# Latent rows of batch 0 between the norm turns of both batches, latent turns under rows, first gate under the rope

## The reference, cut to what matters

```python
h = rms_norm(x, norm_g[1])
proj = h @ w_in                                   # 1024 -> 384 + 256 + 32 + 1024
c_q, c_kv, k_rope, gate = jnp.split(proj, [384, 640, 672], axis=-1)
q  = rms_norm(c_q, q_norm_g) @ w_q_up             # later stage
kv = rms_norm(c_kv, kv_norm_g) @ w_kv_up          # later stage
k_rope = apply_rope(k_rope, cos, sin)
y = o * jax.nn.silu(gate)                         # later stage
```

## Time and profile before

| | us |
|---|---|
| median of 3 runs (1814.23 to 1816.08) | 1815.68 |
| the profiled execution's own time | 1816.16 |
| its span, first to last instruction | 1814.4 |
| `stage_b_in` in it: DVE's first instruction to its last | 1175.65 to 1369.76 |
| PE's first transpose to its last matmul there | 1177.38 to 1364.56 |
| span of PE busy, whole kernel | 1729.9 (95%) |

### The profile page before, as it was taken

How to read it: one execution, slowest core, us unless ns; L and a number is a source line. 1 busy time by engine, 2 the same in 40 slices (tenths; PEclk the granted TensorE clock), 3 DMA queues, 4 the chain that set the end, 5 groups by cost and what they waited for, 6 DMA issues and landing times. The chain is left out here.

```text
span 1814.4 us, 24638 instructions
## 1 busy us (share of the span) xinstructions
PE 1729.9 (95%) x8720; PEld 1462.7 (81%) x8720; DVE 1107.5 (61%) x1974; ACT 726.2 (40%) x1465; POOL 400.8 (22%) x320
## 2 busy tenths in 40 slices
PE   6999999999999999999999999698997999999995
PEld 5888888888888888888888887588786788888883
DVE  5354365456455455455455445544797888888986
ACT  5223223313312322312322322333215877777774
POOL 1001001001001001001000100211004877777774
PEclk9999999999999999999999999898899999999997
DMA  4112112111111112011111110020100000000002
GB/s 162 47 35 70 35 35 70 36 35 58 35 46 58 35 35 68 24 46 58 35 35 70 35 47 1 7 94 1 47 23 27 27 27 26 26 26 26 6 7 110
DMA packets 23241, 76.75 MB, mean 42 GB/s; under 512 B 3088, under 2 KB 3216, under 8 KB 22928
## 3 DMA queue, kind: packets, MB, share of 16 engines
q1 hardware_dynamic: 23184, 75.98, 12.3%
HBM read 71.77 MB, written 4.19 MB: 42 GB/s over the span
## 5 line engine op out<-in xcount | busy, mean ns | idle before, releaser
L754 PE MATMUL bankA<-hTh,wh 128*128 128x512 f32 x1280 | 504.9, 394 | 0.4 <-DVE hTl L504 0.4
L754 PE MATMUL bankA<-hTh,wl 128*128 128x512 f32 x1280 | 498.8, 390 | 0.0
L754 PE MATMUL bankA<-hTl,wh 128*128 128x512 f32 x1280 | 498.8, 390 | 0.0
L754 PEld LDWEIGHTS bankA<-hTh,wl 128*128 128x128 f32 x1280 | 240.4, 188 | 50.9
L754 PEld LDWEIGHTS bankA<-hTh,wh 128*128 128x128 f32 x1280 | 240.7, 188 | 48.3 <-issue 1.1
L754 PEld LDWEIGHTS bankA<-hTl,wh 128*128 128x128 f32 x1280 | 240.8, 188 | 47.0
L304 POOL TENSOR_TENSOR prob<-prob,wt_blk 128x1024 f32<-128x1024 f32 x16 | 32.3, 2022 | 1054.9 <-DVE wt_blk L643 1054.9
L554 DVE TENSOR_TENSOR qk<-bankA,qk 128x512 fp32r<-128x512 f32 x96 | 66.4, 692 | 287.1 <-ACT qk L370 286.9
L370 ACT ACTIVATE qk<-bankA 128x512 fp32r<-128x512 f32 x96 | 57.2, 596 | 366.8 <-PE bankA L754 366.8
L530 DVE TENSOR_TENSOR wl<-raw,wh 128x1024 fp32r<-128x1024 f32 x78 | 103.1, 1321 | 14.5 <-ACT wh L340 12.9
L1475 POOL TENSOR_TENSOR probb<-probb,inv 128x512 f32<-128x512 f32 x96 | 100.0, 1042 | 43.6 <-DVE inv L1666 37.7
(11 more groups left out here) (206 smaller groups left out, 3471.3 us busy)
## 6 DMA issues: line engine op xcount, KB each, us to landing
raw<-a_w_in SPq DMA_DIRECT2D x80, 512.0 KB, 3.3
bias<-alibi SPq DMA_DIRECT2D x8, 512.0 KB, 3.3
raw_out<-a_w_out SPq DMA_DIRECT2D x8, 512.0 KB, 4.1
graw<-b_w_gate SPq DMA_DIRECT2D x8, 512.0 KB, 4.2
raw_o<-b_w_out SPq DMA_DIRECT2D x16, 256.0 KB, 2.6
raw_q<-b_w_q SPq DMA_DIRECT2D x8, 384.0 KB, 3.9
X<-x_prompt SPq DMA_DIRECT2D x4, 512.0 KB, 5.4
X<-x_sample SPq DMA_DIRECT2D x4, 512.0 KB, 8.7
```

Of the source, the lines that this page charges most:

```text
L754: ins = pe.matmul(proj_ps[b][:, :], w[a][:, slot, k * P:(k + 1) * P], hT[c][:, k, b * S:(b + 1) * S], start=(i == 0), stop=(i == last))
```

## The change

PE's new order: norm turns of batch 0; query-latent rows 0 and 1; norm turns 0 to 3 of batch 1; row 2; norm turns 4 to 7 of batch 1; rows 3 to 7; the three query-latent turns of batch 0; all eight key-value rows; gate 0 (of the new order, with both halves); the other seven latent turns; the two rope turns; gates 1 to 7. ACT and DVE follow that order, with one thing to note: what is done with the two halves of gate 0 (exponential, reciprocal, product) stands on both behind the seven other latent turns and the rope's copies. On DVE the rope itself stands ahead of those seven turns.

- The low part of the query-latent weights moves from DVE to POOL, and ACT's split of them from the norm turns of batch 1 to those of batch 0. DVE's first scaling of batch 1 moves from between the norm turns of batch 0 to behind them.
- A row of batch 0 or 1 waits for the norm turns one k at a time (`turn_taken`), not for all eight.
- The weights of the query latent are issued first by SP, the four small tables behind them. The two slots of `graw` go: gate weights are loaded into the part of `gateT` that the gate's own result will take, so the gates run in the order `GATES`, as those parts come free. The first gate's split weights get room of their own behind the key-value weights.

The core of the diff:

```diff
+GATES = (3, 4, 5, 6, 0, 1, 2, 7)
...
-        w = [sb(f"wb{s}", [P, KT * CQ], F32R) for s in "hl"]
+        w = [sb(f"wb{s}", [P, KT * (CKV + B_ROPE) + KT * P], F32R) for s in "hl"]
...
-        latent = scratch[:, 0:NT * CQ].rearrange("p (i c) -> p i c", i=NT)
+        early = sb("early", [P, QT * CQ])
...
-        graw = sb("graw", [P, 2, KT * P])
...
+        gate_at = (KT * widths[1], 0)
...
         @block.sync
         def _(sp):
+            sp.dma_start(raw[:, :], io["b_w_cq"]).then_inc(raw_loaded, 16)
             for dst, name in ((g_col, "g1"), (gq_col, "gq"), (gkv_col, "gkv")):
                 sp.dma_start(dst[:, :], io[name]).then_inc(small_loaded, 16)
             sp.dma_start(rope_tab[:].rearrange("p a j c -> p (a j c)"), io["rope_tok"]).then_inc(small_loaded, 16)
-            sp.dma_start(raw[:, :], io["b_w_cq"]).then_inc(raw_loaded, 16)
-            for n in range(2):
-                sp.dma_start(graw[:, n, :], io["b_w_gate"][n]).then_inc(graw_loaded[n], 16)
...
             sp.wait_ge(w_split, KT)
             sp.dma_start(raw[:, 0:KT * widths[1]], io["b_w_ckv"]).then_inc(raw_loaded, 16)
+            sp.wait_ge(turned, NORM_TURNS)
+            load_gate(3)
...
+            sp.wait_ge(w_split, 2 * KT)
+            load_gate(4)
+            load_gate(5)
+            sp.wait_ge(rope_done, NB)
+            load_gate(6)
+            sp.wait_ge(turned, TR)
+            for n in range(3):
+                load_gate(n)
+            sp.wait_ge(turned, TR + NB)
+            load_gate(7)
...
         @block.gpsimd
...
             pool.memset(key_rope, 0.0).then_inc(zeroed, 1)
+            pool.wait_ge(zeroed, 1)
+            for k in range(KT):
+                cols = slice(k * CQ, (k + 1) * CQ)
+                pool.wait_ge(w_hi, k + 1)
+                pool.tensor_tensor(w[LO][:, cols], raw[:, cols], w[HI][:, cols], ALU.subtract).then_inc(w_split, 1)
...
         @block.scalar
...
+            def split_gate(g):
+                act.wait_ge(graw_loaded[GATES[g]], 16)
+                if g < 2:
+                    act.wait_ge(lat_done, (g + 1) * NT)
+                else:
+                    act.wait_ge(gate_done, 2 * (g - 1))
+                act.activation(gw_all(HI, g), gateT[:, GATES[g], :], ACT.Copy).then_inc(g_hi, 1)
...
+            for k in range(KT):
+                norm_turn(0, k)
+                split_w(0, k)
+            square(0, 0)
+            square(0, 1)
+            for k in range(4):
+                norm_turn(1, k)
+            square(0, 2)
+            for k in range(4, KT):
+                norm_turn(1, k)
+            for i in range(3, NT - 1):
+                square(0, i)
+            act.wait_ge(lat_done, NT)
+            for k in range(KT):
+                split_w(1, k)
+            square(0, NT - 1)
+            for k in range(KQ):
+                latent_turn(0, 0, k)
+            for i in range(NT):
+                square(1, i)
+                if i == 2:
+                    split_gate(0)
+            split_gate(1)
+            for c in range(2):
+                for b in range(NB):
+                    for k in range(ktiles[c]):
+                        if c or b:
+                            latent_turn(c, b, k)
...
         @block.vector
...
+            rate(1)
             scale(0, 0)
             scale(0, 1)
             dve.wait_ge(small_loaded, 64)
             for k in range(KT):
                 norm_turn(0, k)
...
+            dve.wait_ge(rstd_ready, 1)
+            scale(1, 0)
             scale(1, 1)
+            normalize(0, 0)
+            normalize(0, 1)
+            for k in range(4):
+                norm_turn(1, k)
+            normalize(0, 2)
+            for k in range(4, KT):
+                norm_turn(1, k)
+            for i in range(3, NT - 1):
+                normalize(0, i)
+            dve.wait_ge(w_split, KT)
             for k in range(KT):
...
+                split_w(1, k)
+            normalize(0, NT - 1)
+            for k in range(KQ):
+                latent_turn(0, 0, k)
+            for i in range(NT):
+                normalize(1, i)
+                if i == 2:
+                    split_gate(0)
+            split_gate(1)
...
         @block.tensor
...
+                    if c == 0 and i % QT == 0:
+                        pe.wait_ge(turn_taken, i // QT * KT + k + 1)
...
+            norm_turns(0, 0)
+            norm_turns(0, 1)
+            latent_rows(0, 0)
+            latent_rows(0, 1)
+            norm_turns(1, 0)
+            latent_rows(0, 2)
+            norm_turns(1, 1)
+            for i in range(3, NT):
+                latent_rows(0, i)
+            latent_turns(0, 0)
+            for i in range(NT):
+                latent_rows(1, i)
+            gate_rows(0)
+            latent_turns(0, 1)
+            latent_turns(1, 0)
+            latent_turns(1, 1)
             for b in range(NB):
                 pe.wait_ge(rope_done, b + 1)
                 turn(TR + b, [key_rope[:, b * QT + j, :] for j in range(QT)])
...
+            for g in range(1, KT):
+                gate_rows(g)
```

More of the change, by code:

```diff
@@ L964, in stage_b_in @@
         rope_done = sem("b_rope_done")
-        graw_loaded = [sem(f"b_graw_loaded{i}") for i in range(2)]
+        graw_loaded = [sem(f"b_graw_loaded{i}") for i in range(KT)]
         g_hi = sem("b_g_hi")
@@ L977, in stage_b_in, with gw, gw_all, latent @@
         TR = TKV + NB * KKV
-        gw = [t[:, 0:2 * KT * P].rearrange("p (s c) -> p s c", s=2) for t in w]
+        gate_at = (KT * widths[1], 0)
+        def gw(part, g, k):
+            at = gate_at[g % 2] + k * P
+            return w[part][:, at:at + P]
+        def gw_all(part, g):
+            return w[part][:, gate_at[g % 2]:gate_at[g % 2] + KT * P]
+        def latent(c, i):
+            wide, j = (CQ, CKV)[c], i % QT
+            if i < QT:
+                return early[:, j * wide:(j + 1) * wide]
+            at = c * QT * CQ + j * wide
+            return scratch[:, at:at + wide]
         block = ctx.enter_context(nc.Block())
@@ new lines, in norm_turns, with latent_rows @@
+            def norm_turns(b, c):
+                pe.wait_ge(x_scaled, 2 * b + c + 1)
+                for k in range(c * KT // 2, (c + 1) * KT // 2):
+                    turn(b * KT + k, [scaled_x[:, j, k * P:(k + 1) * P] for j in range(QT)])
+            def latent_rows(c, i):
+                n = c * NT + i
+                if n >= 4:
+                    pe.wait_ge(lat_taken, n - 3)
+                for k in range(KT):
+                    if c == 0 and i % QT == 0:
+                        pe.wait_ge(turn_taken, i // QT * KT + k + 1)
+                    pe.wait_ge(w_split, c * KT + k + 1)
+                    for m, (a, z) in enumerate(SPLIT_PRODUCT):
+                        ins = pe.matmul(proj_ps[n % 4][:, 0:widths[c]], hT[a][:, k, i * P:(i + 1) * P],
+                                        w[z][:, k * widths[c]:(k + 1) * widths[c]],
+                                        start=(k == 0 and m == 0), stop=(k == KT - 1 and m == 2))
+                ins.then_inc(lat_done, 1)
@@ new lines, in latent_turns, with gate_rows @@
+            def latent_turns(c, b):
+                pe.wait_ge(lat_taken, c * NT + (b + 1) * QT)
+                for k in range(ktiles[c]):
+                    turn((TQ, TKV)[c] + b * ktiles[c] + k,
+                         [latent(c, b * QT + j)[:, k * P:(k + 1) * P] for j in range(QT)])
+            def gate_rows(g):
+                pe.wait_ge(g_split, g + 1)
+                for b in range(NB):
+                    m = 2 * g + b
+                    if m < 4:
+                        pe.wait_ge(lat_taken, 2 * NT - 3 + m)
+                    else:
+                        pe.wait_ge(gate_taken, m - 3)
+                    for k in range(KT):
+                        for q, (a, z) in enumerate(SPLIT_PRODUCT):
+                            ins = pe.matmul(proj_ps[m % 4][:, :], gw(a, g, k),
+                                            hT[z][:, k, b * S:(b + 1) * S], start=(k == 0 and q == 0),
+                                            stop=(k == KT - 1 and q == 2))
+                    ins.then_inc(gate_done, 1)
```

137 lines of the change are left out of this document (32 added, 105 removed).

## The result

Side by side on one chip the changed kernel took **1799.76 us** (median; 1798.98 to 1800.72) and the kernel before 1815.55: a ratio of 0.9917, interval 0.9905 to 0.9929, or 15.8 us less. The forecast was 1802.3, within 1797 to 1808.

What follows compares the result with a forecast made beforehand. PE, busy 95% of the span, was taken as the bound, so gains come from its pauses and half-clock stretches. 8.7 us up to gate 0, then 97.3 instead of 101.9, made 13.4 less: 1802.3 us, range 1797 to 1808.

Steps and rivals of the forecast that it cites:

- the forecast's own account: Whole kernel: the part-by-part sum comes true, 1802.3 us with its own range 1800 to 1805; chance 0.42.
- the warmer rival: Clock holds in the new wait and row 0 is fed faster: 2.5 to 5 us less, 1797.3 to 1799.8; chance 0.27.
- The start: Stage's start: weights land at about 1182.1, tables 0.3 us later, ACT starts at 1182.5; POOL's subtractions are not held up.
- Row 0: First query row: entered at 1187.8, 5.4 us earlier than before, and ending at 1194.4.
- the middle price of a cold start: 2.5 us for starting at 1.2 GHz, the middle of 1.1, 2.5 and 3.5; added at row 0 and after the new wait.
- the prediction's lower bound: Row 0: POOL's last subtraction ends at 1191.3, three more matmuls follow, so the row ends no earlier than 1191.8.
- Rows 1 to 7, the turns among them, the key-value rows: After row 0: rows and eight turns take 32.8 us; three query turns 1.5, then key-value rows 25.2, unbroken.
- Nine turns: Between gates 0 and 1: seven latent and two rope turns take 5.5 us at DVE's pace; gate 1 starts at 1270.2.
- The colder rival: Nine turns leave the clock low, gate 1 costs 3.5 us more, row 0 3.5 instead of 2.5: 1806.8; chance 0.18.
- The new wait: Ahead of gate 2: PE waits 2.8 us, once, for DVE's split; 2.5 us of low clock follow.
- the sum of 13.4: Total gain: 8.7 us up to gate 0's start, then 97.3 us instead of 101.9, with 0.1 of rounding.

Runs made afterwards that it cites:

- the run with the front as before: Changed kernel with small tables issued before the query weights, low parts on DVE, all 16 norm turns ahead of row 0: 1801.07 us, ratio 0.9926.
- the run with pieces: Changed kernel with table `g1` issued first, query weights in four pieces behind it, other small tables last: 1794.39 us, ratio 0.9892.

## Why the prediction was right, point by point

The measured 1799.76 lies within the stated range, but just below the 1800 to 1805 of the forecast's own account and at the upper end of the warmer rival.

**The start: right.** ACT's first copy waited for the last table, behind the weights:

```profile
gateT<-b_w_cq SPq DMA_DIRECT2D x1, 1536.0 KB, 6.4
rope_tab<-rope_tok SPq DMA_DIRECT2D x1, 64.0 KB, 4.8
...
1180.60 0.69 ACT L1060 ACTIVATE hTbh<-bankB,gb_col 128x512 fp32r<-128x512 f32 x1 [7.32 <-DMA rope_tab<-rope_tok]
1181.84 7.87 POOL L1041 TENSOR_TENSOR wbl<-gateT,wbh 128x384 fp32r<-128x384 f32 x8 [5.63 <-ACT wbh L1053]
```

The weights landed 6.4 us after the stage's start, the table, issued at 2.3, at 7.1: 0.7 behind, where 0.3 was taken from the earlier trace rows. Those rows give 0.7 too: the smaller transfer was issued 0.4 us later (1197.73, and 1197.36 for the larger), which the 0.3 leaves out. POOL's eight subtractions took 7.87, one each 0.98, at ACT's pace (a single one took 1.01, where 0.96 was taken by proportion); that they would not be held up by the norm turns was right. The turns on DVE, with one operand from a bank, took the usual 0.75, and the eight scalings behind them 3.86, where eight took 3.26 before: the first, beside POOL's last piece, took 1.08, the others 0.48 at most. In the run with the low parts on DVE, without that piece, none of these eight took more than 0.48. As forecast, that cost nothing. The rule of the Trainium skill's page "GPSIMD Engine Reference" ("Key points"), that POOL contends with DVE instructions in a two-port mode or with two memory inputs, leaves the turns free, and the trace agrees; whether the scaling that was held ran in such a mode no run shows.

**Row 0: the term that was mis-sized.** "I take 4.13 and the middle price of a cold start, 2.5: 1194.4", that is 18.8 after the start. It was 17.0, and the later steps kept those 1.8 us. The clock was not low under row 0; two windows over the last turns and the first matmuls of the row:

```profile
1184.00:1185.00 1.00, 1.00 (x6) 0.72 (x4) 0.76 (x2) 1.00 (x3) 1.00 (x2) 0.50 0.00 0
1186.00:1187.00 1.00, 1.00 (x8) 1.00 (x7) 0.76 (x2) 1.00 (x3) 1.00 (x2) 1.00 0.00 0
```

Turns 4 to 7, one each 0.98 us, kept PE at work, and the rise came under the last of them. So row 0 was bound by its feeding instead. POOL ended its last piece at 1189.71 (1181.84 + 7.87), 16.2 after the start, where the prediction's lower bound had 15.7 from the same feed; PE waited 0.2 for it, and the last three matmuls put the end at 17.0. The prediction had both numbers and took the wrong one. The price of 2.5 was that of the key-value rows; the query rows themselves had paid 1.1 in its own sums. And the kernel before shows where the low clock under row 0, 1192 to 1195 in the earlier trace rows, came from:

```profile
1188.00:1189.00 1.00, 0.00 (x0) 0.00 (x0) 1.00 (x3) 1.00 (x3) 0.00 (x0) 1.00 0.00 0
...
1190.00:1191.00 1.00, 0.66 (x4) 0.42 (x4) 1.00 (x3) 1.00 (x3) 0.00 (x0) 1.00 0.00 0
1191.00:1192.00 1.00, 0.71 (x4) 0.48 (x4) 1.00 (x3) 0.95 (x2) 0.00 (x0) 0.78 0.00 0
```

It had been 1.00 since 1181.5 and fell under the turns of batch 1, with PE idle before them and for a third of each microsecond among them. Just these turns no longer stand ahead of row 0, and the price went with them; where they were put back, in the run with the front as before, row 0 started at 0.50 again.

**Rows 1 to 7, the turns among them, the key-value rows: right.** 32.6 us against 32.8, and 27.0 against 26.7 with the three turns. PE's waits show no turn that waited there.

**Nine turns: right,** 5.28 against 5.5, with one wait of 0.3 for the first bank. The colder rival had them leave the clock low. The window over them stands at 1.00 above, and gate 1 started at full clock. The Trainium skill's page "TensorE: Matmul & The Clock Gate" ("Part 4: PE-mode transpose") says that transposes don't count as PE work for the clock in the same way; over these turns, 36 transposes with PE busy for 4.73 of 5.20 us at 1.00, the trace doesn't agree (whether they run in the mode that the page means, no row shows).

**The new wait: right in place, cause and number of times** (2.39 against 2.8; DVE's two halves of gate 0 stood ahead of the split, and PE went on at 1279.86, when it was done):

```profile
1270.15 3.35 DVE L1244 RECIPROCAL gateT<-gateT 128x512 f32<-128x512 f32 x1
...
1274.59 3.35 DVE L1244 RECIPROCAL gateT<-gateT 128x512 f32<-128x512 f32 x1
...
1278.59 1.22 DVE L1175 TENSOR_TENSOR wbl<-gateT,wbh 128x1024 fp32r<-128x1024 f32 x1
```

What followed it cost 1.9, where 2.5 was taken between 0 and 3.5. That the middle came near is luck: the run with pieces, in which the same wait cost only 0.35 more, shows that it can go either way, and nothing in the prediction decided which.

So the sum of 13.4 became 15.4 by two terms, 1.8 at row 0 and 0.6 behind the new wait, less small ones (the wait was 0.4 shorter, the gates took 0.5 longer). Of the warmer rival one half came true (row 0), the other not.

**What the sum hid.** It had the pause ahead of gate 0 vanish because gate 0 stands over the rope, and of the two early splits it named only the second, as work "in PE's pause" that now lies under the gate. The runs turn that round: with the splits early, gate 0 in its old place loses 0.9; with the splits late, PE's old order loses 5.4 more. The total was right, and its attribution wrong: the early place of the first two gates' splits on ACT and DVE, which got no term of its own, was worth as much as the largest move on PE.

## What to carry to other kernels

When work of the bounding engine is moved over a pause, look for the wait that the same helper engine will now cause a step later: here half a gate's postprocessing ahead of a split cost a wait of 2.4 us and 1.9 us behind it, and moving that split by one half gave it all back. Undo the parts of a change together as well as singly: the two moves of PE's work gave back only 6.0 of an expected 13.1 us, and 5.4 of the rest lay in where ACT and DVE split the gates' weights, not in PE's order. Issue what the first instruction needs first, and feed a stage's first rows in pieces: with its table behind a whole weight block ACT began at 7.07 us, where it had begun at 3.32 before, and with the table ahead and the weights in pieces at 3.06.

## What the runs showed of the hardware

The same wait of PE, 2.36 to 2.5 us, was followed by a granted clock of 0.50 for some 3 us in the changed kernel, in its repetition, and with the front, the query turns or the low parts as before, and by 1.00 throughout in the kernel with the weights in pieces. What decides wasn't found, nor, with one profile of each kernel but one, whether it is the same in every execution; what follows such a wait cost 0.35 or 1.9 us here.

From issue to landing a table of 64 KB took 2.0 us ahead of the weights and 4.8 behind them.
